# First attention: q and k as high and low parts, scores as three fp32r products, k turned before q

## What is computed

```python
qa = apply_axial_rope(rms_heads(qa.reshape(b, s, 8, 64), q_gain), cos, sin)
ka = apply_axial_rope(rms_heads(ka.reshape(b, s, 2, 64), k_gain), cos, sin)
va = va.reshape(b, s, 2, 64)
ya = gqa_axial_attention(qa, ka, va) @ w_branch_a

def one_block(q_blk):                  # 128 queries
    logits = jnp.einsum('bqkgd,bskd->bkgqs', q_blk, k) * 64 ** -0.5
    p = jax.nn.softmax(logits, axis=-1)
    return jnp.einsum('bkgqs,bskd->bqkgd', p, v)
```

## Time and profile before

| | us |
|---|---|
| median of 3 runs | 1366.95 |
| lowest and highest run | 1366.62, 1370.09 |
| span of the profiled execution | 1366.5 |
| TensorE (PE) busy | 1260.3 |
| DVE busy | 708.9 |
| ACT busy | 632.9 |
| GpSimd (POOL) busy | 351.5 |

### The profile page before, as it was taken

How to read it: one execution, slowest core, us unless ns; L and a number is a source line. 1 busy time by engine, 2 the same in 40 slices (tenths; PEclk the granted TensorE clock), 3 DMA queues, 4 the chain that set the end, 5 groups by cost and what they waited for, 6 DMA issues and landing times.

```text
span 1366.5 us, 19228 instructions
## 1 busy us (share of the span) xinstructions
PE 1260.3 (92%) x7198; PEld 1032.7 (76%) x7199; DVE 708.9 (52%) x896; ACT 632.9 (46%) x856; POOL 351.5 (26%) x295
## 2 busy tenths in 40 slices
PE   5999899999999999899999998599999999999970
PEld 4888767788879888767788877477788878778860
DVE  4233367321566333367321566677746575874556
ACT  4232466422323222476422323577645565774445
POOL 0532000000110332000000110257735554884330
PEclk9999999999999999999999998699999999999995
DMA  6842200034364222200024364479977887996326
GB/s 214 265 130 93 93 1 2 1 97 150 100 239 155 93 93 93 93 1 2 1 93 151 98 244 153 149 228 312 343 217 227 294 266 232 323 345 219 92 48 247
DMA packets 65339, 211.74 MB, mean 155 GB/s; under 512 B 14359, under 2 KB 14871, under 8 KB 64471
## 3 DMA queue, kind: packets, MB, share of 16 engines
q1 hardware_dynamic: 50492, 178.32, 38.1%
q0 software_dynamic: 12192, 24.00, 7.1%
q10 hardware_dynamic: 2592, 8.53, 1.6%
HBM read 200.13 MB, written 34.25 MB: 172 GB/s over the span
## 4 chain that ended last, share of the span: by engine, by line
PE 75%; DVE 8%; issue 5%; ACT 4%; DMA 3%; POOL 3%; SPq 0%; ACTq 0%; POOLq 0%; DVEq 0%
PE banks L702 20%; PE banks L704 20%; PE banks L703 20%; PE banks L868 2%; PE banks L832 2%; DMA moe_raw<-in_expert_w 2%; PE banks L903 2%; DVE moe_lo L1405 2%; PE banks L910 2%; PE banks L985 1%; PE banks L843 1%; POOL gated L602 1%; PE banks L736 1%; ACT moe_hi L1251 1%; PE banks L1010 1%
## 5 line engine op out<-in xcount | busy, mean ns | idle before, releaser
L1251 ACT ACTIVATE moe_hi<-moe_raw 128x2048 fp32r<-128x2048 f32 x102 | 195.1, 1917 | 54.7 <-PE banks L704 31.2
L1424 DVE TENSOR_TENSOR wlo<-raw,whi 128x2048 fp32r<-128x2048 f32 (+1 forms) x52 | 116.0, 2231 | 184.5 <-ACT whi L1094 184.5
L1405 DVE TENSOR_TENSOR moe_lo<-moe_raw,moe_hi 128x2048 fp32r<-128x2048 f32 x86 | 195.0, 2290 | 19.8 <-ACT moe_hi L1251 19.7
L702 PE MATMUL banks<-xT,whi 128*128 128x512 f32 x448 | 175.9, 393 | 0.0
L703 PE MATMUL banks<-xT,whi 128*128 128x512 f32 x448 | 175.5, 392 | 0.0
L704 PE MATMUL banks<-xT,wlo 128*128 128x512 f32 x448 | 175.4, 391 | 0.0
L602 POOL TENSOR_TENSOR gated<-gated,kqv 128x512 f32<-128x512 f32 x16 | 25.4, 1602 | 496.6 <-DVE kqv L1566 496.6
L702 PE MATMUL banks<-moe_lo,xeh 128*128 128x512 f32 x368 | 146.7, 399 | 4.9 <-DVE xel L1788 3.1
L702 PE MATMUL banks<-wlo,xT 128*128 128x256 f32 (+1 forms) x448 | 135.4, 302 | 13.2 <-DVE wlo L1424 13.2
L703 PE MATMUL banks<-moe_hi,xeh 128*128 128x512 f32 x368 | 145.0, 394 | 0.0
L704 PE MATMUL banks<-moe_hi,xel 128*128 128x512 f32 x368 | 144.9, 394 | 0.0
(11 more groups left out here) (262 smaller groups left out, 2317.9 us busy)
## 6 DMA issues: line engine op xcount, KB each, us to landing
moe_raw<-in_expert_w SPq DMA_DIRECT2D x192, 512.0 KB, 5.7
raw<-in_front_w SPq DMA_DIRECT2D x104, 512.0 KB, 4.5
toeplitz_rows<-bias_rows POOLq DMA_DIRECT2D x4, 1152.0 KB, 13.7
kqv<-in_x_turned SPq DMA_DIRECT2D x8, 512.0 KB, 8.0
pt<-in_x SPq DMA_DIRECT2D x2, 2048.0 KB, 10.1
x_rows<-pt ACTq DMA_DIRECT2D x8, 512.0 KB, 2.7
token_sums<-pt ACTq DMA_DIRECT2D x8, 512.0 KB, 3.7
sum_tile<-token_sums SPq DMA_DIRECT2D x8, 512.0 KB, 6.5
```

Of the source, the lines that this page charges most:

```text
L702: mm(dst, left[0], right[1], start=first, stop=False)
L1251: A(moe_hi[m % SPLIT_E], moe_raw[m % RAW_E], ACT.Copy).then_inc(e_hi, 1)
L1405: V.tensor_tensor(moe_lo[m % SPLIT_E], moe_raw[m % RAW_E], moe_hi[m % SPLIT_E].bitcast(F32), ALU.subtract).then_inc(lo_sem(m % ECH), 1)
L1424: V.tensor_tensor(view(lo, shape), view(raw[c % 2], shape), view(hi, shape).bitcast(F32), ALU.subtract).then_inc(w_split, 1)
```

## The change

k is transposed and released first, then the four q tiles. Of each tile two parts are kept: ACT copies the bank as fp32r (the high part), then DVE subtracts the high part from the bank (the low part) and raises the new semaphore qkA_lo. The bank is released, and the scores may begin, by qkA_lo. In scores, each head's fp32 product is replaced by three fp32r products that add up in the bank: q high by k low, high by high, q low by k high. The two heads alternate within each of the three. The low part of k uses the sixth piece of qkvA, the low part of q lies over outB0 and outB1.

```diff
--- before.py
+++ after.py
@@ -70,7 +70,7 @@
     for _t in range(TT):
         if _s > 0 and _t == 0:
             TR_ORDER += [("x1", _s - 1, TT - 1, f) for f in range(2)]
-    TR_ORDER += [("q", _s, _t) for _t in range(TT)] + [("k", _s, u) for u in range(2)]
+    TR_ORDER += [("k", _s, u) for u in range(2)] + [("q", _s, _t) for _t in range(TT)]
     TR_ORDER += [("x1", _s, _t, f) for _t in range(TT if _s == SEQS - 1 else TT - 1) for f in range(2)]
 assert MM_N % 4 == 0 and N_CHUNK % 2 == 0
 
@@ -129,7 +129,7 @@
 
     if key[0] == "x1":
         return "x1T_ready", 2 * TT * key[1] + 2 * key[2] + key[3] + 1 + 2
-    return "qkA_ready", (TT + 2) * key[1] + (TT if key[0] == "k" else 0) + key[2] + 1
+    return "qkA_lo", (TT + 2) * key[1] + (0 if key[0] == "k" else 2) + key[2] + 1
 
 
 FREE_PER = {}
@@ -287,6 +287,7 @@
         vA_t = place("vA", TT * 2 * VW)
         kqv_at = arena_base + at[0]
         kqv = place("kqv", 12 * SEQ + TT * 12 * VW)
+        qkvA_at = arena_base + at[0]
         qkvA = place("qkvA", 6 * SEQ)
         prob = place("prob", 3 * 768)
         pt = place("pt", 8 * SEQ)
@@ -298,8 +299,10 @@
         x_stage = [kqv[:, (2 + t) * D:(3 + t) * D] for t in range(TT)]
         sg = kqv[:, 0:16 * SEQ].rearrange("p (f n) -> p f n", f=16)
         lnp = kqv[:, 0:2 * D].rearrange("p (a n) -> p a n", a=2)
-        qA = qkvA[:, 0:4 * SEQ].rearrange("p (m n) -> p m n", m=4)
-        kA = qkvA[:, 4 * SEQ:5 * SEQ]
+        q_lo = nc.alloc_sbuf_tensor_at("q_lo", [P, 4 * SEQ], F32R, offset=outB_at)[:, :]
+        qk_hi = nc.alloc_sbuf_tensor_at("qk_hi", [P, 6 * SEQ], F32R, offset=qkvA_at)[:, :]
+        qA = [t.rearrange("p (m n) -> p m n", m=4) for t in (qk_hi[:, 0:4 * SEQ], q_lo)]
+        kA = [qk_hi[:, i * SEQ:(i + 1) * SEQ] for i in (4, 5)]
         vA = vA_t.rearrange("p (t v d) -> p t v d", t=TT, v=2)
 
         gated_at = arena_base + at[0] - 4 * (8 * SEQ + 3 * 768 + 6 * SEQ)
@@ -390,8 +393,8 @@
         q_copied, q_square, q_var, q_root, q_normed, q_turned = [
             sem(n) for n in ("q_copied", "q_square", "q_var", "q_root", "q_normed", "q_turned")]
         pool_step = sem("pool_step")
-        q_mult, qkA_ready, va_ready, b_act, b_dve = [sem(n) for n in
-                                                     ("q_mult", "qkA_ready", "va_ready", "b_act", "b_dve")]
+        q_mult, qkA_ready, qkA_lo, va_ready, b_act, b_dve = [sem(n) for n in
+                                                             ("q_mult", "qkA_ready", "qkA_lo", "va_ready", "b_act", "b_dve")]
         a_max, a_exp, t_done, pt_act, pt_dve, den_ready, den_turned, den_kept, o_done, pv_hi, pv_lo = [
             sem(n) for n in ("a_max", "a_exp", "t_done", "pt_act", "pt_dve", "den_ready", "den_turned", "den_kept", "o_done", "pv_hi",
                              "pv_lo")]
@@ -425,7 +428,7 @@
 
         by_name = {"q_copied": q_copied, "va_ready": va_ready, "b_act": b_act, "b_dve": b_dve,
                    "gate_ready": gate_ready, "yb_used": yb_used, "ya_used": ya_used, "residual": residual, "xlo": xlo,
-                   "qkA_ready": qkA_ready, "x1T_ready": x1T_ready}
+                   "qkA_lo": qkA_lo, "x1T_ready": x1T_ready}
 
         def den_of(p, v):
 
@@ -805,18 +808,18 @@
                 pe.wait_ge(tab_dve, N_TAB // 2)
                 pe.wait_ge(q_turned, s * 3 + 3)
                 pe.wait_ge(ident_in, 16)
+                for u in range(2):
+                    b = tr_open(("k", s, u))
+                    for v in range(2):
+                        last = nc.tensor.transpose(b[:, v * P:(v + 1) * P], k_rot[:, 2 * u + v, :], ident)
+                    last.then_inc(tr_done, 1)
                 for t in range(TT):
                     b = tr_open(("q", s, t))
                     for m in range(4):
                         last = nc.tensor.transpose(b[:, m * P:(m + 1) * P],
                                                    q_rot[:, t, m].rearrange("p v d -> p (v d)"), ident)
                     last.then_inc(tr_done, 1)
-                for u in range(2):
-                    b = tr_open(("k", s, u))
-                    for v in range(2):
-                        last = nc.tensor.transpose(b[:, v * P:(v + 1) * P], k_rot[:, 2 * u + v, :], ident)
-                    last.then_inc(tr_done, 1)
-                pe.wait_ge(qkA_ready, s * 6 + 6)
+                pe.wait_ge(qkA_lo, s * 6 + 6)
                 pe.wait_ge(va_ready, s * TT + TT)
                 pe.wait_ge(b_act, s * 12 + 12)
                 pe.wait_ge(b_dve, s * 12 + 12)
@@ -828,9 +831,10 @@
                         t, m = p // GROUP, p % GROUP
                         if p >= 2:
                             pe.wait_ge(a_exp, s * N_EXP + exps_by(p - 1))
-                        for v in range(2):
-                            last = mm(bank[score_bank(p, v)][:, :], qA[halves[v], m, t * P:(t + 1) * P], kA[halves[v], :],
-                                      start=True, stop=True)
+                        for n, (i, j) in enumerate(((0, 1), (0, 0), (1, 0))):
+                            for v in range(2):
+                                last = mm(bank[score_bank(p, v)][:, :], qA[i][halves[v], m, t * P:(t + 1) * P], kA[j][halves[v], :],
+                                          start=(n == 0), stop=(n == 2))
                         last.then_inc(sc_done, 1)
                         return
                     t, hp = (p - NPA) // 2, p % 2
@@ -1156,14 +1160,12 @@
                     if c + 2 < N_CHUNK:
                         split_hi(c + 2)
                 act.wait_ge(tab_out, 16)
+                for u in range(2):
+                    b = tr_wait(("k", s, u))
+                    A(kA[0][:, u * 256:(u + 1) * 256], b[:, 0:256], ACT.Copy).then_inc(qkA_ready, 1)
                 for u in range(TT):
                     b = tr_wait(("q", s, u))
-                    A(qA[:, :, u * P:(u + 1) * P], b.rearrange("p (m n) -> p m n", m=4), ACT.Copy) \
-                        .then_inc(qkA_ready, 1)
-                for u in range(2):
-                    b = tr_wait(("k", s, u))
-                    A(kA[:, u * 256:(u + 1) * 256], b[:, 0:256], ACT.Copy) \
-                        .then_inc(qkA_ready, 1)
+                    A(qA[0][:, :, u * P:(u + 1) * P], b.rearrange("p (m n) -> p m n", m=4), ACT.Copy).then_inc(qkA_ready, 1)
 
                 def keep_turned(p):
                     act.wait_ge(t_done, s * N_TURN + turns_by(p) + 1)
@@ -1478,6 +1480,19 @@
                     if c + 2 < N_CHUNK:
                         split_lo(c + 2)
 
+                def turned_lo(key, lo, hi, src):
+                    i = TR_ORDER.index(key)
+                    n = s * (TT + 2) + (0 if key[0] == "k" else 2) + key[2]
+                    dve.wait_ge(qkA_ready, n + 1)
+                    V.tensor_tensor(lo, src(bank[i % 2]), hi.bitcast(F32), ALU.subtract).then_inc(qkA_lo, 1)
+
+                for u in range(2):
+                    cols = slice(u * 256, (u + 1) * 256)
+                    turned_lo(("k", s, u), kA[1][:, cols], kA[0][:, cols], lambda b: b[:, 0:256])
+                for u in range(TT):
+                    cols = slice(u * P, (u + 1) * P)
+                    turned_lo(("q", s, u), qA[1][:, :, cols], qA[0][:, :, cols], lambda b: b.rearrange("p (m n) -> p m n", m=4))
+
                 def logits_of(p):
                     k = 2 * (p % 2)
                     if p < NPA:
```

## The result

The changed kernel takes 1377.42 us (median of 7 runs, 1371.71 to 1380.86) against 1366.95 (1364.73 to 1370.09): ratio 1.0066, 95% interval 1.0052 to 1.008. It is slower by 10.5 us; 1378.5 was forecast.

What follows compares the result with a forecast made beforehand. TensorE was taken as the bound, carrying the chain for 75% of the span. Later score starts less product gains gave +2.9 us, the low clock +8.6: 1366.95 + 11.5 = 1378.5 us, range 1369 to 1385.

Steps and rivals of the forecast that it cites:

- Where the scores start: Turning stage: q transposes queue behind DVE's weight split and low parts; scores start at 167.44 instead of 163.32, +4.1 us.
- The gain of the products: Score products: three side-by-side fp32r twos take 0.88 instead of 1.06 us, gaining 0.18 us per head pair (0.16 to 0.215).
- Rival D: Score groups: the 0.20 us at start and end goes with fp32, so not slower than before, 1366.8; chance 0.06.
- The sum with the clock held: Turning stage and scores: later start less product gain, clock unchanged, +1.45 us a sequence, +2.9 us in all.
- The clock: Turning stage into attention loop: TensorE's clock falls in both sequences, +4.3 us each (3.5 to 5.2), +8.6 in all.
- my bounds (low until 3.3 us or more into dense work): Attention loop: the low clock lasts 3.3 to 6.8 us into dense work, half lost, 1.7 to 3.4 us a sequence.
- B: Turning stage: the clock holds in both sequences, 1370 us (1368.5 to 1371.5); chance 0.12.
- C: Score products: the two heads' fp32r products don't run side by side, 1399 with low clock, 1390 without; chance 0.12.
- its form with exposed loads: Score products: each two waits for its own weight loads, 0.19 us each, 17 us more; shares a chance of 0.12.

Runs made afterwards that it cites:

- e3: The changed kernel with TensorE kept busy by unread products in the idle pieces of the turning stage, waits kept: 1369.98 us.
- e4: The changed kernel with the split of chunk 13 moved behind both attentions on ACT and DVE: 1364.6 us.
- e9: e3 with each head's scores as one fp32 product of the high parts, low parts made but unused: 1376.11 us.
- e5: The changed kernel without low parts, bank released by ACT, scores as three equal fp32r high-part products, k's high part divided by three: 1363.76 us.
- e10: The changed kernel run again with nothing altered, on the same chip as the others: 1376.81 us.
- e1: The changed kernel with its turning stage kept, but each head's scores as one fp32 product of the high parts: 1379.37 us.
- e6: e4 with all three score products of head 0 queued before those of head 1, instead of alternating: 1366.19 us.
- e8: The kernel before with only k turned and copied ahead of q, all fp32, bank released by ACT: 1368.73 us.

## Why the prediction was right

**Where the scores start.** Worked out: 167.44 with the clock held, 168.6 with it low. Measured: 167.49 in e3 with its head start taken out; 168.14 and 168.64 in the two executions of the changed kernel. The steps between agree as well (in e3, with the 1.08 added: q0's transposes 162.76 for 162.74, ACT's copy 163.45 for 163.44). e4 shows the cause that was named, the queue behind DVE's split, for 3.5 of the 4.2 us.

**The gain of the products.** Worked out: 0.18 a head pair (0.17 for the first), 15 counting pairs a sequence, 2.7 in all, from a full-height fp32r row and the assumption that half-height ones pair like fp32. Measured: 0.16 a pair (3.11 to 2.95), 2.4 a sequence (e9 less e3), 2.1 to 2.2 in e5. Slightly over-sized: 0.90 instead of 0.88 a group. Rival D, that the 0.20 at start and end goes with fp32, is out: 0.90 less 3 x 0.23 leaves 0.21.

**The sum with the clock held.** +1.45 a sequence worked out, +1.8 measured (e3); in runs +2.9 worked out and +2.9 measured (1369.98 against 1367.06).

**The clock.** +4.3 a sequence was worked out for the low clock, so +5.75 in all; e10 shows +5.8 and +5.7. That these agree to a tenth is in part luck. Over e3, e10 has 4.0 a sequence, not 4.3: scores start 1.2 later (168.64 - 158.10 = 10.54 for 9.36; 1.2 worked out), from there to the first turns it takes 0.7 longer (3.78 for 3.10; 0.6 worked out), and 2.1 are left for the dense work (2.5 worked out). The 0.3 too much here covers the 0.35 too little of the sum with the clock held.

The profiled execution of the changed kernel has +2.5 and +5.1: there the fall in the first sequence was over by 166.44, before the scores began, which my bounds (low until 3.3 us or more into dense work) didn't allow for. Of the six stages of this form (the changed kernel, e10, e1), three lie inside these bounds; in e1 one fall ended 1.3 us into the dense work and one before the scores. That is the one step that was too narrow. The runs from 1371.71 to 1380.86, with a lower mean granted clock in the longer ones on the whole, fit it, which is argued and not shown run by run. That the clock is a cost of its own and not a side effect of the waiting is shown by e3, where the waits on DVE stay and 7 us go. The Trainium skill (TensorE: Matmul & The Clock Gate, HAM oscillation) has the next burst starting slow after a wait; the traces agree here, with 0.50 granted after 4.23 us without work. The falls in e4, e6 and e8 came with no idle piece over 1.84 us.

**A reading that did no harm.** The prediction took the span of the profiled execution and the median run as 0.45 us apart. Wherever both are on record for one execution, the span is 1.7 us below the run's time, so the profiled execution of the kernel before was not the median one. The forecast was added to the median and isn't touched by it.

**The rivals.** B was the price without the fall: e3 measured it at 1370 as stated. C is out, since six products group in twos (0.90, not 1.56), and its form with exposed loads too. The Trainium skill (TensorE: Matmul & The Clock Gate, Part 3) has a load overlap a running product only in other row groups; by the prediction's sum that would have made the group 0.57 us longer, and the traces don't show it (0.90).

## What to carry to other kernels

Splitting an operand into high and low parts adds a second engine to the release of a bank; look at what that engine has queued at that moment, and move what nobody needs soon behind it, or give the transposes more banks, before judging the cheaper products. A stage of transposes and copies between two dense stages is also where the clock can fall, so a delay there can cost about twice its length: in e10 the scores' start, 4.2 us later by the waits, cost up to 4.0 us more by the clock. When an experiment leaves out part of the arithmetic, count the data-dependent work behind it (here the experts' products) before reading its time.

## What the runs showed of the hardware that I had not expected

Products of half height (64 of the 128 rows) of two heads pair up although three of one head are queued before those of the other (e6: 2.95 us a head pair, as with alternation). The low clock after the same idle piece of 4.2 us lasted 3.4, 13.7, 17.1 and 17.1 us in four stages of the same program; where it ended before the scores it cost 0.7 us (2.5 against 1.8), where it reached into the loop 3.3 to 4.0. It also fell in second sequences without such a piece, where TensorE was idle for at most 1.41 us (e4, e6) or 1.84 us (e8) at a time.
